# Query section of the second layer multiplied inside the last expert group of the first, from the partial sums

## The reference

```python
for l in range(DEPTH):                                  # 2 layers
    u = rms_norm(x, norm_mix_g[l]) @ w_in[l]            # aq, ak, av, bq, bf, bi, bg, cb, cc, cx: 3328 columns
    o_a = differential_attention(aq, ak, av, ...)       # aq: the first 512 columns
    o_b = hgrn2(bq, bf, bi, bg, ...)
    o_c = short_conv(cb, cc, cx, conv_w[l])
    x = x + concat(o_a, o_b, o_c) @ w_out[l]
    h = rms_norm(x, norm_ffn_g[l])
    x = x + hier_moe(h, ...)                            # 32 experts, each token goes to 2 of them
```

## Time and profile before

| what | value |
|---|---|
| median of 3 runs | 1173.14 us (1172.86 to 1174.67) |
| profiled execution | a separate execution; the page gives its span, 1171.5 us, and no time of its own beside it |
| granted TensorE clock, mean | 0.903 |
| busy: PE, DVE, ACT, POOL | 888.0, 464.3, 173.0, 43.3 us |
| DMA | 442.23 MB, 377 GB/s over the span |
| chain that ended last | PE 50%, DMA 42%, DVE 4% |

### The profile page before, as it was taken

One profiled execution on the slowest core, in us unless ns is written; L12 is line 12 of the kernel. 1 busy time (PEld: TensorE's weight loads), 2 busy tenths in 40 slices (PEclk: granted clock), 3 DMA queues, 4 the chain that ended last, 5 costly groups with the idle time before them and its releaser, 6 DMA issues.

```text
span 1171.5 us, 20439 instructions
## 1 busy us (share of the span) xinstructions
PE 888.0 (76%) x8553; PEld 534.2 (46%) x8553; DVE 464.3 (40%) x1247; ACT 173.0 (15%) x483; POOL 43.3 (4%) x98
## 2 busy tenths in 40 slices
PE   9999998675657565748799999976566666566577
PEld 6577475342424232425465675743323333333244
DVE  2977474332323232313238664734223223232232
ACT  2334121100000000100113441211000000000001
POOL 2001120000000000000000120000000000000000
PEclk9999998887979897988899999998979797988789
DMA  8946589999999999999997275999999999999997
GB/s 280 387 192 244 223 349 428 427 426 427 429 427 429 427 429 429 429 429 424 412 386 286 73 271 185 393 427 427 427 427 429 429 429 428 429 427 429 429 425 299
DMA packets 56141, 442.23 MB, mean 377 GB/s; under 512 B 9472, under 2 KB 12560, under 8 KB 31248
## 3 DMA queue, kind: packets, MB, share of 16 engines
q1 hardware_dynamic: 56080, 441.37, 91.1%
HBM read 440.30 MB, written 1.05 MB: 377 GB/s over the span
## 4 chain that ended last, share of the span: by engine, by line
PE 50%; DMA 42%; DVE 4%; issue 2%; SPq 1%; POOL 0%; ACT 0%; DVEq 0%; POOLq 0%
DMA ring<-in_expert_w_up 40%; PE psum L885 14%; PE psum L918 8%; PE psum L927 6%; PE psum L1002 5%; PE psum L899 4%; PE psum L858 2%; PE psum L763 2%; DMA work<-in_expert_w_down 2%; PE psum L1019 1%; DVE work L1546 1%; PE psum L950 1%; SPq L477 1%; PE psum L1170 1%; PE psum L1128 1%
## 5 line engine op out<-in xcount | busy, mean ns | idle before, releaser
L885 PE MATMUL psum<-ring,work 128*32 128x256 f32 x3712 | 261.7, 443 | 108.3 <-DMA ring<-in_expert_w_up 107.5
L885 PEld LDWEIGHTS psum<-ring,work 128*32 128x32 f32 x3712 | 146.7, 127 | 221.5 <-issue 174.9
L899 PE MATMUL psum<-ring,work 128*32 128x256 f32 x1664 | 126.1, 455 | 126.4 <-DVE work L1552 126.0
L1544 DVE TENSOR_SCALAR work<-work 128x128 f32<-128x128 f32 x62 | 14.5, 233 | 340.3 <-ACT work L1216 340.3
L899 PEld LDWEIGHTS psum<-ring,work 128*32 128x32 f32 x1664 | 56.8, 127 | 190.7 <-DVE work L1552 148.7
L1557 DVE COPY work<-psum 32x256 f32<-32x256 f32 x124 | 52.6, 424 | 139.6 <-PE psum L899 138.4
L918 PE MATMUL psum<-ring,hT 128*128 128x512 f32 x224 | 98.0, 593 | 0.0
L1220 ACT ACTIVATE work<-psum 32x256 f32<-32x256 f32 x124 | 46.2, 373 | 270.5 <-PE psum L899 269.8
L1216 ACT ACTIVATE work<-psum 128x128 f32<-128x128 f32 x62 | 17.2, 277 | 363.5 <-PE psum L885 335.7
L927 PE MATMUL psum<-hT,ring 128*128 128x256 f32 x320 | 70.7, 379 | 0.0
L858 PE MATMUL psum<-work 128*128 128x512 f32 x112 | 55.4, 640 | 15.1 <-DVE work L1557 15.1
(11 more groups left out here) (300 smaller groups left out, 796.1 us busy)
## 6 DMA issues: line engine op xcount, KB each, us to landing
ring<-in_expert_w_gate SPq DMA_DIRECT2D x64, 2048.0 KB, 18.1
ring<-in_expert_w_up SPq DMA_DIRECT2D x60, 2048.0 KB, 22.5
ring<-in_expert_w_down SPq DMA_DIRECT2D x52, 2048.0 KB, 22.4
ring<-in_w_in SPq DMA_DIRECT2D x10, 2048.0 KB, 17.3
work<-in_expert_w_down SPq DMA_DIRECT2D x6, 2048.0 KB, 14.2
ring<-in_w_out SPq DMA_DIRECT2D x4, 2048.0 KB, 8.2
ring<-in_w_in SPq DMA_DIRECT2D x8, 512.0 KB, 12.0
maps<-in_expert_w_down SPq DMA_DIRECT2D x2, 2048.0 KB, 9.0
```

Source lines behind the costliest of these rows:

```text
L885: last = T.matmul(bank[GU_BANK[i % 2]][CAP * j:CAP * j + CAP, 0:2 * P], xg[:, k, CAP * i:CAP * i + CAP], gate_up[:, :, k, P * j:P * j + P] ...
L899: last = T.matmul(bank[5][CAP * q:CAP * q + CAP, 0:2 * P], actT[i % 2][:, CAP * j:CAP * j + CAP], down[j][:, 2 * P * q:2 * P * q + 2 * P], ...
```

## The change

In layer 0 the query section of layer 1 is multiplied within the last expert group. After group 6 the banks hold x plus the outputs of 28 experts; the last four are missing. Since the projection is linear and the norm's factor is applied afterwards, the kernel now

- copies the banks to x (`sums_to_x`, ScalarE), transposes x (`sums_transposed`) into `hT` with layer 1's gain, and multiplies by the query weights (`project_ahead`), one token tile behind unit 0 and one behind unit 1; ScalarE keeps the two results in `part_q`;
- puts x back into the sum banks (`seeds_again`), since the copy closed them;
- sends each of the four last experts' outputs (32 token slots) through the same weights (`project_rest`): VectorE transposes it and applies the gain (`output_transposed`), and the product, 32 rows by 512, goes to `rest`;
- at the start of layer 1 scatters `rest` with the gate matrix (`scatter_rest`, two matmuls), and VectorE adds `part_q`.

The units of that group run up 0, down 0, up 1, down 1, up 2, down 2, and the `keep_warm` matmuls are gone from it. The query weights go to the buffer `maps`, and are issued behind unit 0's loads of the last group. Group 6 stands outside the loop in layer 0. Layer 1's last group is as it was. At the start of layer 1 all 16 transposes come first, and L1023's two matmuls go between the halves of `bq`.

```diff
+
+        part_q = [u[:, 9, :], u[:, 11, :]]
+        yT = h[:, 0, :, :]
+        rest = h[:, 1, 0:4, :].rearrange("p a n -> p (a n)")
+        flat = h[:, 1, 5:7, :].rearrange("p a n -> p (a n)")
...
+
+        def first_tiles(l):
+
+            first = slot(IN_MAPS) if l else ring[:, SECTIONS[AQ][2], :]
+            return first.rearrange("p (k n) -> p k n", k=KT)
 
...
                 for i in range(UG - 1):
                     unit(ring_full, main, last, i, (GROUPS - 1) * UG + i, LAST, 3)
+                    if i == 0 and l < DEPTH - 1:
+                        first_section(l + 1)
                 sg, su, sd = placed(l, LAST[UG - 1])
...
+                ahead = l < DEPTH - 1
+                Waq = first_tiles(l + 1)
+
+                def sums_transposed():
+
+                    for n in range(4):
+                        t, half = n // 2, n % 2
+                        if n < 2:
+                            e.wait_ge(S.gat_sb.sem, S.gat_sb.after(turn, 1))
+                            e.wait_ge(S.xg_ok.sem, S.xg_ok.after(turn, 2))
+                        else:
+                            e.wait_ge(ahead_t_sb.sem, ahead_t_sb.after(l, n - 1))
+                        e.wait_ge(ahead_x.sem, ahead_x.after(l, 2 * t + 2))
+                        rows = x[:, t, :].rearrange("p (c k) -> p k c", k=KT)
+                        for k in range(4):
+                            last = T.transpose(bank[AHEAD_BANK[half]][:, k * P:k * P + P], rows[:, 4 * half + k, :], ident[:, :])
+                        last.then_inc(ahead_t_ps.sem, 1)
+
+                def seeds_again():
+
+                    for n in range(4):
+                        T.matmul(bank[SUM_BANK[n]][:, :], ident[:, :], x[:, n // 2, n % 2 * 512:n % 2 * 512 + 512], start=True, stop=False)
+
+                def project_ahead(t):
+
+                    if t == 0:
+                        e.wait_ge(ahead_t_sb.sem, ahead_t_sb.after(l, 4))
+                    else:
+                        e.wait_ge(ahead_q_sb.sem, ahead_q_sb.after(l, 1))
+                    for k in range(KT):
+                        if t == 0 and k % 2 == 0:
+                            e.wait_ge(early_part[k // 2].sem, early_part[k // 2].after(l + 1, 16))
+                        last = T.matmul(bank[7][:, :], hT[:, k, t * P:t * P + P], Waq[:, k, :], start=(k == 0), stop=(k == KT - 1))
+                    last.then_inc(ahead_q_ps.sem, 1)
+
+                def project_rest(n):
+
+                    e.wait_ge(yt_ok.sem, yt_ok.after(l, n + 1))
+                    for k in range(KT):
+                        for q in range(4):
+                            last = T.matmul(bank[GU_BANK[n % 2]][CAP * q:CAP * q + CAP, 2 * P:3 * P], yT[:, k, CAP * n:CAP * n + CAP],
+                                            Waq[:, k, P * q:P * q + P], start=(k == 0), stop=(k == KT - 1))
+                    last.then_inc(rest_ps.sem, 1)
+
                 gathered(S, turn)
                 gate_transposes(S, turn, True)
-                expert_units(S, turn, LAST_TURN[0:3], slots, loaded)
-                e.wait_ge(S.gat_sb.sem, S.gat_sb.after(turn, 1))
-                keep_warm(4, 7)
-                expert_units(S, turn, LAST_TURN[3:5], slots, loaded)
-                keep_warm(2, 7)
-                expert_units(S, turn, LAST_TURN[5:], slots, loaded)
+                if ahead:
+                    sums_transposed()
+                    for n in range(UG - 1):
+                        expert_units(S, turn, [("up", n), ("down", n)], slots, loaded)
+                        if n < TI:
+                            project_ahead(n)
+                            project_rest(n)
+                    seeds_again()
+                else:
+                    expert_units(S, turn, LAST_TURN[0:3], slots, loaded)
+                    e.wait_ge(S.gat_sb.sem, S.gat_sb.after(turn, 1))
+                    keep_warm(4, 7)
+                    expert_units(S, turn, LAST_TURN[3:5], slots, loaded)
+                    keep_warm(2, 7)
+                    expert_units(S, turn, LAST_TURN[5:], slots, loaded)
                 i = UG - 1
...
+                if ahead:
+                    project_rest(UG - 2)
 
...
-            def experts(S, turn, order, slots, loaded):
+                if ahead:
+                    project_rest(UG - 1)
...
                     i, half = n // 2, n % 2
                     T.matmul(bank[SUM_BANK[n]][:, :], gatT[:, i * P:i * P + P], ye[:, half * 512:half * 512 + 512],
-                             start=False, stop=False).then_inc(S.scat_ps.sem, 1)
+                             start=False, stop=final).then_inc(S.scat_ps.sem, 1)
 
             def expert_units(S, turn, order, slots, loaded, first_group=False):
 
...
+                def scatter_rest(t, name):
+
+                    T.matmul(bank[PROJ_BANK[name]][:, :], gatT[:, t * P:t * P + P], rest[:, :], start=True, stop=True).then_inc(proj_ps.sem, 1)
+
+                if l:
+                    stream_ready(e, l, 1)
+                    transposed_rows(1, x[:, 1, :].rearrange("p (c k) -> p k c", k=KT))
+                    e.wait_ge(rest_sb.sem, rest_sb.after(l - 1, UG))
+                    scatter_rest(0, "aq0")
+                    scatter_rest(1, "aq1")
+                    e.wait_ge(ht_sb.sem, ht_sb.after(l, 4))
+                    W = section(B)
+                    project_columns(W, "bq", 0, rstd_by_column)
...
-                with e.Fori(2, GROUPS - 1) as g:
+                more = l < DEPTH - 1
+                with e.Fori(2, GROUPS - 2 if more else GROUPS - 1) as g:
                     experts(main, l * GROUPS + g, IN_TURN, later, turn_loaded(g))
+                if more:
+                    experts(main, l * GROUPS + GROUPS - 2, IN_TURN, later, turn_loaded(GROUPS - 2), final=True)
                 count, prior = extra_groups(e, l)
                 with e.If(count > 0):
...
+            def sums_to_x(done):
+
+                for n in range(4):
+                    A(x[:, n // 2, n % 2 * 512:n % 2 * 512 + 512], bank[SUM_BANK[n]][:, :], ACT.Copy).then_inc(done.sem, 1)
+
             def last_experts(l, turn):
 
                 S, i = main, UG - 1
+                ahead = l < DEPTH - 1
+
+                def rest_out(n):
+
+                    e.wait_ge(rest_ps.sem, rest_ps.after(l, n + 1))
+                    for q in range(4):
+                        last = A(rest[CAP * n:CAP * n + CAP, P * q:P * q + P], bank[GU_BANK[n % 2]][CAP * q:CAP * q + CAP, 2 * P:3 * P], ACT.Copy)
+                    last.then_inc(rest_sb.sem, 1)
+
+                if ahead:
+                    e.wait_ge(S.scat_ps.sem, S.scat_ps.after(turn - 1, 4))
+                    sums_to_x(ahead_x)
                 e.wait_ge(S.gat_ps.sem, S.gat_ps.after(turn, 1))
                 A(gat_both, bank[7][:, :], ACT.Copy).then_inc(S.gat_sb.sem, 1)
-                expert_units(S, turn, LAST_TURN)
+                if ahead:
+                    for n in range(UG - 1):
+                        expert_units(S, turn, [("up", n)])
+                        e.wait_ge(S.ye_ps.sem, S.ye_ps.after(turn, n + 1))
+                        if n:
+                            e.wait_ge(yt_ok.sem, yt_ok.after(l, n))
+                        A(flat[0:P // 2, :], bank[5][0:P // 2, 0:2 * P], ACT.Copy).then_inc(flat_ok.sem, 1)
+                        expert_units(S, turn, [("down", n)])
+                        if n < TI:
+                            e.wait_ge(ahead_q_ps.sem, ahead_q_ps.after(l, n + 1))
+                            A(part_q[n], bank[7][:, :], ACT.Copy).then_inc(ahead_q_sb.sem, 1)
+                            rest_out(n)
+                else:
+                    expert_units(S, turn, LAST_TURN)
                 e.wait_ge(gate_ps.sem, gate_ps.after(l, 1))
                 A(sil[i % 2], bank[LAST_GU[0]][:, 0:P], ACT.Exp, scale=-1.0).then_inc(S.gu_exp.sem, 1)
+                if ahead:
+                    rest_out(UG - 2)
                 e.wait_ge(S.ye_ps.sem, S.ye_ps.after(turn, UG))
                 A(ye_last[0:P // 2, :], bank[5][0:P // 2, 0:2 * P], ACT.Copy).then_inc(S.ye_act.sem, 1)
                 for t in range(TI):
                     e.wait_ge(tail_ps.sem, tail_ps.after(l, t + 1))
                     A(x[:, t, 512:1024], bank[SUM_BANK[2 * t + 1]][:, :], ACT.Copy).then_inc(taken_act.sem, 1)
+                if ahead:
+                    rest_out(UG - 1)
 
             def expert_units(S, turn, order):
 
...
-                expert_units(S, turn, LAST_TURN, c)
+                ahead = l < DEPTH - 1
+                ca = Chain(dve_ahead, l)
+
+                def output_transposed(n, rows):
+
+                    tile = yT[:, :, CAP * n:CAP * n + CAP]
+                    V.transpose(tile, rows.rearrange("p (m k) -> p k m", k=KT)).then_inc(ca.step(), 1)
+                    e.wait_ge(ca.sem, ca.last())
+                    TT(tile, tile, gmix[:, l + 1, :].unsqueeze(2).to_broadcast([P, KT, CAP]), ALU.mult).then_inc(yt_ok.sem, 1)
+
+                if ahead:
```

(30 more changed lines are left out.)

85 lines of the change are left out of this document (52 added, 33 removed).

## The result

| | kernel before | changed kernel |
|---|---|---|
| median of 5 runs, us | 1173.51 (1172.86 to 1175.44) | 1189.19 (1186.58 to 1191.94) |
| ratio, 95% interval | | 1.0135 (1.0123 to 1.0148) |
| profiled execution's span, us | 1171.5 | 1184.9 |
| TensorE busy, us | 888.0 | 894.5 |
| last scatter of layer 0 ends | 584.95 | 609.0 |

The account below looks back on a forecast made before the run. TensorE was taken to bound layer 0's last expert group, with little room for added work. +20.8 in the group, -11.5 at the boundary and +1.5 for the clock gave +10.8 us, so 1183.9 us, range 1176 to 1191.

Parts of the forecast that it names:

- its two large terms: Layer 0's last group ending 20.8 us later, and 11.5 us saved at the boundary to layer 1.
- Added less displaced in the last group: Layer 0's last expert group: 34.1 us added on TensorE, 13.1 displaced, so its last scatter ends 20.8 us later.
- the 8.2: Layer 0's last group: three activations of 2.73 us between up and down leave TensorE idle, 8.2 us added.
- The boundary: Last scatter of layer 0 to layer 1's state-query projection: 18.8 us becomes 7.3, saving 11.5.
- The 1.5 charged for the clock: At the layer boundary: 1.5 us of the 1.7 lost to a slow granted clock was expected to be lost again.
- The clock at the new gaps: Layer 0's last group: downs after three new gaps run slowly, about 0.5 us each, +1.5 (0 to +4.5).
- a shift at the boundary goes to the end one for one: After the boundary everything is tied to TensorE, so the shift at 603.78 equals the shift at the end.
- TensorE's busy time: Sign in the profile after: TensorE busy rises by about 14 us, less slow clock.
- The DMA side: Query weights loaded ahead of unit 29's loads: unit 31's weights 5.4 us later, but no TensorE wait and no queue hole.
- Rival A: Layer 0's last group: TensorE's idle time while weights stream swallows the added work, about 1165 us; chance 0.07.
- Rival B: Before layer 0's last group: the loop's end caused TensorE's idle stand, so 6.9 us come back, 1177; chance 0.08.
- Rival C: Layer 0's last group: more straight-line code brings one more pair of idle stands, 7.9 us, about 1192; chance 0.08.

Follow-up runs that it names:

- The reordered kernel: Changed kernel with its last group's projections and outputs placed between each unit's up and down, same matmuls: 1180.33 us, ratio 1.0061 to the kernel before.

## Why the prediction was right

The forecast's mechanism, a last group that TensorE bounds, is what the trace shows, and its two large terms were sized well. That the median still lies in the range is in part luck: it is 5.3 above the forecast and 1.8 below the upper bound, and two of the five runs are beyond it. Half of the 5.3 is read in the traces below, the other half is the median above the profiled execution. Point by point:

- *Added less displaced in the last group*: +20.8 foreseen, 74.3 - 52.3 = +22.0 measured. The projections took 7.06 and 7.06 (6.87 said), the outputs 1.88 each (1.8), the residual 3.63 (3.5), the sums' transposes, from the end of the gate transposes to the first gate and up, 3.4 (3.2), each activation gap 2.73 (2.73). The reordered kernel got back 7.1 of the 8.2 by filling the gaps, the one without the residual 2.95 of 3.5. (The reason given for putting x back, that the copy had closed the banks, is not shown: it is the flag of group 6's scatter that closes them, and no run here goes on without closing and refilling.)
- *The boundary*: 7.3 foreseen, 5.6 measured and 0.45 for the two small matmuls inside the projection (behind which the shift is 11.25), so 12.8 saved for 11.5. The 1.5 charged for the clock did not come: 1.00 was granted over 608.9 to 614.6. The section that went was the one that had run slowly (4.69 for 8), and its clock loss went with it.
- *The clock at the new gaps*: +1.5 foreseen, 0 measured; the three downs took 1.93. The term was wrong by all of its size. These two, some 2.8 too much, are hidden in the sum by the next point.
- *What the prediction did not have*: the last group was entered 2.1 later (534.73 against 532.62), 0.7 by unit 27's weights (518.60 against 517.90) and 1.4 by its down, which took 3.29 from 526.67, not 1.93. The change need not be the cause: the kernels with the early load alone and with the loop kept entered it at 534.68 and 535.28, and all others but one between 532.8 and 535.2. And layer 1 added 2.15 to the 11.25. Of that 0.3 had come when unit 30's weights were there (1156.04 against 1144.51), 2.4 came with the gate and up behind the wait (5.87 against 3.48), and 0.5 went again in unit 31, where the kernel before waited and ran slowly too. The sum of the spans is 13.4 where 10.8 was foreseen. So by its own sign the step "a shift at the boundary goes to the end one for one" failed, by 2.15: 0.3 in the stream, and the rest in the last group of layer 1, where the pair of stands had become one wait for weights with slow matmuls behind it. It held within 0.8 for the four kernels with the loop kept (the section left out at the boundary: 9.57 and 8.9; the early load alone: 4.5 and 4.9).
- *TensorE's busy time*, another sign: about +14 less slow clock was said, +6.5 came (888.0 to 894.5), and -0.8 in the second trace (887.2). It is a poor sign: the same instructions were busy 888.0 before and 893.6 with the straight line in layer 1.
- *The DMA side*: as foreseen; the queue was held 23.52 (21.94 said), no hole, no wait. Loaded early without work to cover it, the same 2 MB cost 5.8; not loaded at all, they gave nothing back.
- *Rival A* (the work fits) is out: no weights are waited for in the group after 518.6. (Its 1165 took 13.5 off at the boundary where the forecast had 11.5; with that it is 1167.) *Rival B* (the stand goes with the loop's end) is out: 4.43 after 4.48, and 4.71 where only the loop's end was moved. The Trainium skill, Advanced Engine Details and Errata, section ISA Cache, says that an engine holds its instructions in few, large lines; what the prediction drew from it, a stand at a jump and none in a straight run, fits the stand that stayed at the jump, and not the ones of the next point.
- *Rival C* (more stands for code) was given 0.08 and put at the wrong place and price. The long straight run of the last group shows none over 0.65 (one of 1.45 in the kernel without the residual). But there is one of 1.77 at the start of layer 1's first group. All six kernels with group 6 in a straight line in layer 0 have one there (1.09 to 2.43 in seven traces), and those with the loop kept or with the straight line in layer 1 none over 0.6, beside one of 2.0 before the group's last down that every kernel has. (The smaller of them say little alone: at the start of layer 0's first group the changed kernel had 0.52 in one trace and 1.33 in the other.) That one edit cost 5.0 us when it stood alone and 3.6 when it was taken back.

What is open: why unit 30's weights came 3.0 late in the kernel with the straight-line group 6 alone, with the DMA engines full; why a straight line before the last group puts a stand in the next layer's first group; why the pair of stands before layer 1's last group is in two kernels and one stand in the others; why the kernels enter the last group of layer 0 up to 2.7 apart (532.6 to 535.3). The trace counts a DMA queue for instructions (44 packets before, 50 after, 45 with the loop kept), which fits stands for code. But it doesn't tie a packet to a stand, and the kernel with the straight line in layer 1 has 47 without one.

The kernel that came closest keeps the loop, orders the projections over the activations, and leaves the residual out of the banks. It equals the kernel before: its last scatter ends 13.1 later (598.04 against 584.95) and its boundary is 13.2 shorter. 2.7 of the 13.1 are its late entry into the group (535.28). No run here beat both kernels with the whole computation in it.

## What to carry to other kernels

Work moved into a stretch that waits for data is free only as far as that stretch's idle time goes; add up the gaps of exactly that stretch, not the engine's share over the phase, and put the moved work into the gaps by its order, which was worth about half of the loss here. A loop made a straight line to give one turn of it another flag is a change of its own, and should be timed alone: here it cost 5.0 us, and it was no term of the sum. When a part is cut out to measure it, what it covered comes back: the two cuts gave 60% and 73% of what their own instructions took.

## What the runs showed that was not expected

- The same instructions in a straight line instead of a loop's last turn: +5.0 us (ratio 1.0037), with weights 3.0 late in the group behind it and a stand of 1.37 some 220 us later. Closing matmuls of bfloat16 zeros, 512 columns, let the loop stay, at 0.27 each (0.81 for three; the fourth has no record).
- A stand of 4.0 to 5.9 us lies before each last group in every kernel without the closing matmuls. With the four of them ahead of it 3.56 and 3.79 remained: 4.43 from the scatter's end (535.28) to the gather (539.71), within what it is without them. The stand hid them, though the 12 transposes behind the jump were not hidden.
- A wait of 4.2 to 6.6 us for unit 30's weights in the last group of layer 1 is followed by a gate and up of 5.2 to 6.4 instead of 3.66, in ten traces (the granted clock over 1156 to 1162 of the changed kernel is 0.59). The gap of 2.73 before a down goes either way: 1.93 three times in the changed kernel's last group of layer 0, but 3.29 and 3.61 for the last down of group 6 in its two layers, and 3.42 in the kernel with most of the projection left out.
- Kernels with the change spread over 2.7 to 6.8 us between 4 to 11 executions; the kernel before over 4.1 in 27.
